# Hybrid pool/SSD decoder step: weight rings placed on 256-byte bounds, sample z values kept beside the x rows

## The reference

```
proj = einsum('bld,dk->blk', h, w_in)            # -> u | z | xBC | dt | gates
branch A = pooled(u) -> w_pool -> w_pool_br
xs, bm, cm = causal_conv(xBC);  y = ssd_chunked(xs, dt, a, bm, cm, state)
y = (y + d_skip * xs) * silu(z);  y = grouped RMSNorm(y) * ssd_norm_w
branch B = y @ w_ssd_br
merged = sigmoid(g_pool) * A + sigmoid(g_ssd) * B
x = LN(ALPHA*x + merged @ w_out);  x = LN(ALPHA*x + memory attention)
x = LN(ALPHA*x + (silu(x @ w_gate) * (x @ w_up)) @ w_down)
```

## Time and profile before

| | |
|---|---|
| median of 3 runs | 2116.43 us (2116.13 to 2117.07) |
| the profiled execution | 2115.2 us |
| its span, first to last instruction | 2113.6 us |
| PE busy | 2094.5 us, 99% |
| weight loads on PE | 2077.5 us, 98% |
| DVE, ACT, POOL busy | 1480.1, 1118.3, 162.4 us |
| granted TensorE clock | 0.997 over the span |

### The profile page before, as it was taken

How to read it: one execution, slowest core, us unless ns; L and a number is a source line. 1 busy time by engine, 2 the same in 40 slices (tenths; PEclk the granted TensorE clock), 3 DMA queues, 4 the chain that set the end, 5 groups by cost and what they waited for, 6 DMA issues and landing times.

```text
span 2113.6 us, 47660 instructions
## 1 busy us (share of the span) xinstructions
PE 2094.5 (99%) x17400; PEld 2077.5 (98%) x17400; DVE 1480.1 (70%) x2394; ACT 1118.3 (53%) x1671; POOL 162.4 (8%) x298
## 2 busy tenths in 40 slices
PE   9999999999999999999999999999999999999997
PEld 8999999999999999999999999999999999999997
DVE  8788877888788988544446876976666666545545
ACT  6566556566545545434344455666666665433333
POOL 1000000000002332000000010001111110000000
PEclk9999999999999999999999999999999999999998
DMA  7555555455557998555555575468888887555553
GB/s 284 194 172 184 189 187 184 164 184 189 186 194 245 310 290 274 178 179 180 179 180 204 178 278 209 160 220 289 281 291 285 277 286 253 172 189 180 180 181 110
DMA packets 125363, 451.78 MB, mean 214 GB/s; under 512 B 16057, under 2 KB 16313, under 8 KB 124233
## 3 DMA queue, kind: packets, MB, share of 16 engines
q1 hardware_dynamic: 101232, 366.41, 50.9%
q0 software_dynamic: 24048, 84.20, 13.0%
HBM read 427.87 MB, written 23.99 MB: 214 GB/s over the span
## 4 chain that ended last, share of the span: by engine, by line
PE 94%; DVE 3%; ACT 1%; DMA 1%; issue 1%; ACTq 0%; POOL 0%; DVEq 0%; SPq 0%
PE G L402 26%; PE G L403 26%; PE G L404 26%; PE M L402 4%; PE M L403 4%; PE M L404 4%; DVE sb_wlo L1398 1%; PE M L514 1%; PE M L526 1%; DMA sb_raw<-in_wstream 0%; ACT sb_whi L871 0%; DVE sb_resid L1682 0%; PE M L517 0%; PE M L497 0%; ACT sb_resid L1370 0%
## 5 line engine op out<-in xcount | busy, mean ns | idle before, releaser
L1398 DVE TENSOR_TENSOR sb_wlo<-sb_raw,sb_whi 128x1024 fp32r<-128x1024 f32 x688 | 834.3, 1223 | 566.0 <-ACT sb_whi L871 563.3
L871 ACT ACTIVATE sb_whi<-sb_raw 128x1024 fp32r<-128x1024 f32 x688 | 721.6, 1059 | 745.5 <-PE G L404 624.7
L402 PE MATMUL G<-sb_xH,sb_whi 128*128 128x264 f32 (+1 forms) x3072 | 871.4, 284 | 2.2 <-DVE sb_wlo L1398 1.6
L403 PE MATMUL G<-sb_xL,sb_whi 128*128 128x264 f32 (+1 forms) x3072 | 868.3, 283 | 0.0
L404 PE MATMUL G<-sb_xH,sb_wlo 128*128 128x264 f32 (+1 forms) x3072 | 867.9, 283 | 0.0
L402 PEld LDWEIGHTS G<-sb_xH,sb_whi 128*128 128x128 f32 x3072 | 577.1, 188 | 5.0 <-issue 2.5
L403 PEld LDWEIGHTS G<-sb_xL,sb_whi 128*128 128x128 f32 x3072 | 577.3, 188 | 0.0
L404 PEld LDWEIGHTS G<-sb_xH,sb_wlo 128*128 128x128 f32 x3072 | 577.2, 188 | 0.0
L403 PE MATMUL G<-sb_hL,sb_whi 128*128 128x264 f32 x704 | 200.2, 284 | 0.0
L404 PE MATMUL G<-sb_hH,sb_wlo 128*128 128x264 f32 x704 | 199.7, 284 | 0.0
L402 PE MATMUL G<-sb_hH,sb_whi 128*128 128x264 f32 x704 | 199.3, 283 | 0.0
(11 more groups left out here) (383 smaller groups left out, 2955.5 us busy)
## 6 DMA issues: line engine op xcount, KB each, us to landing
sb_raw<-in_wstream SPq DMA_DIRECT2D x688, 512.0 KB, 4.1
sb_st<-in_state_ssd POOLq DMA_DIRECT2D x32, 512.0 KB, 5.9
out_new_ssd_s<-sb_st POOLq DMA_DIRECT2D x32, 512.0 KB, 3.8
sb_tmp<-in_state_ssd POOLq DMA_DIRECT2D x34, 256.0 KB, 5.1
sb_cumbc<-scr_cum POOLq DMA_DIRECT2D x8, 1024.0 KB, 5.0
sb_resid<-in_state_ssd POOLq DMA_DIRECT2D x30, 256.0 KB, 4.4
sb_kc<-in_kc POOLq DMA_DIRECT2D x8, 512.0 KB, 8.2
sb_vc<-in_vc POOLq DMA_DIRECT2D x8, 512.0 KB, 6.1
```

The lines of the kernel that those rows point to most:

```text
L402: pe.matmul(out, w, kH, start=start, stop=False)
L403: pe.matmul(out, w, kL, start=False, stop=False)
L871: act.activation(whi[:, slot, :], raw[:, slot, :], ACT.Copy).then_inc(hi_ready, 1)
L1398: dve.tensor_tensor(wlo[:, slot, :], raw[:, slot, :], whi[:, slot, :].bitcast(F32), ALU.subtract)\
```

## The change

The three weight rings move up by 128 bytes, so that every tile in them begins at 0 modulo 256; another 128 bytes are left free behind them, so that x rows keep their place at 128 modulo 256. Everything behind moves by 256 bytes and keeps its place modulo 256. The 256 bytes are found by taking away `zsamp` as a tensor (1,024 bytes): its values go to columns `GAP + 32` to `GAP + 47` of the `xL` rows, the last 16 of the 320. The DVE copy and the DVE multiply that touch it take the layout of `dtxc` and `decc`.

```diff
+        alloc(ctx, "before_weights", [P, 32])
         raw = alloc(ctx, "raw", [P, RING, UNIT])
         whi = alloc(ctx, "whi", [P, RING, UNIT], F32R)
         wlo = alloc(ctx, "wlo", [P, RING, UNIT], F32R)
+        alloc(ctx, "before_x", [P, 32])
...
+        zsamp = planes[:, KT:2 * KT, GAP + 8 * XPG:GAP + 12 * XPG]
...
-        xsamp, zsamp, tails, bcp = overlay(
-            KEEP, xsamp=([P, SG, XPG],), zsamp=([P, SG, XPG],), tails=([P, CT, 11],), bcp=([P, SG],))
-        CS, prod = overlay(KEEP + 2 * XPG * SG * 4, CS=([P, SG, XPG],), prod=([P, XPG, P],))
-        (rc,) = overlay(KEEP + 3 * XPG * SG * 4 + 3 * P * 4, rc=([P, 4, 16],))
+        xsamp, tails, bcp = overlay(
+            KEEP, xsamp=([P, SG, XPG],), tails=([P, CT, 11],), bcp=([P, SG],))
+        CS, prod = overlay(KEEP + XPG * SG * 4, CS=([P, SG, XPG],), prod=([P, XPG, P],))
+        (rc,) = overlay(KEEP + 2 * XPG * SG * 4 + 3 * P * 4, rc=([P, 4, 16],))
...
-                        dve.tensor_copy(rows(zsamp), zs[:, :, SEQ:T])
+                        dve.tensor_copy(own_rows(zsamp), zs[:, :, SEQ:T].rearrange("p i (r b) -> p i r b", r=2))
...
-            dve.tensor_tensor(CS[:, :, :], CS[:, :, :], zsamp[:, :, :], ALU.mult).then_inc(s["sy_ready"], 1)
+            dve.tensor_tensor(cs_rows, cs_rows, zsamp[:, :, :], ALU.mult).then_inc(s["sy_ready"], 1)
```

More of the change, by code:

```diff
@@ L1588, in group @@
                 gr = t["g"].now() * 2
-                own_rows = dtxc[:, gr:gr + 2, :] if isinstance(gr, int) else dtxc[:, bass.ds(gr, 2), :]
-                dve.tensor_tensor(own_rows.rearrange("p r (b i) -> p i r b", i=XPG),
+                own_rows = (lambda x: x[:, gr:gr + 2, :].rearrange("p r (b i) -> p i r b", i=XPG)) if isinstance(gr, int) else (
+                    lambda x: x[:, bass.ds(gr, 2), :].rearrange("p r (b i) -> p i r b", i=XPG))
+                dve.tensor_tensor(own_rows(dtxc),
                                   sl[:, :, 0:NSAMP].rearrange("p i (r b) -> p i r b", r=2),
```

## The result

The changed kernel takes 2135.03 us (median of 4 runs, 2134.78 to 2135.63), the kernel before beside it 2116.28 us (4 runs, 2115.76 to 2117.07): 18.75 us more, ratio 1.0089 with a 95% interval of 1.0077 to 1.0101. It is slower, by two thirds of what I forecast.

A forecast was written before the change was run, and what follows sets the result against it. PE, busy 99% of the span, was taken as the bound. The profiled 2115.2 us plus 27.5 for x plus 0 gave 2142.7, with the median 1.2 above: 2144 us, 1.3% slower; range 2091 to 2155, the forecast's own 2125 to 2161.

The forecast's parts named there:

- The bound: Whole kernel: PE is busy 99% of the span, so time is the number of matmuls times the distance between their starts.
- What counts is the place against the weight tile: Main forecast for x matmuls: rows half of 256 bytes from the weight tiles stream slower; 2144 us, chance 0.48.
- y's slow rows moved four along: Sign in y's matmuls: rows 1 and 2 become slow, 5 and 6 fast, the average staying 122.5 ns.
- The rival of the row's own place: Rival for x: only the moving row's place modulo 256 counts, so the time stays 2116.4 us; chance 0.13.
- that of the tile's own place: Rival: weight tiles at 0 touch fewer 256-byte pieces, so y, mix and h gain too; 2100 us, sharing 0.39 for faster.
- The rule: PE's weight and row ports are independent, so the weights' place could not change x's streaming: median 2116.4 us.
- The price, 123.3 ns: Time per x matmul after the change, taken from y row 6 (row at 0, weights at 128).
- The term, 27.5 us: Added time for x: 10,560 matmuls times 123.3 less 120.7 ns.
- the base: x's time per matmul before the change, taken as 120.7 ns for all, with the input projection in the middle.
- settles in a rhythm: Condition for being wrong: x at one place for thousands of matmuls finds a rhythm that six matmuls of y never show.
- y, mix and h at nothing, mem below 1 us: Other PE matmuls: y, mix and h taken as 0, bound 6 us either way; 384 of memH and memL, 1 us.
- The helping rival, 2091 us: Rival for x: streams meet less often, x goes at 118.3 ns, -25 us; faster by either way had chance 0.39.

The follow-up runs named there:

- both_zero: The changed kernel without the second 128-byte gap, so weight tiles and x rows both begin at 0 modulo 256; 2116.07 us against 2115.72 for the kernel before.
- probe_map: The kernel before plus 65 unused stretches of 96 matmuls, at 64 pairs of high-row and low-row distances from the weight tiles; 128/128 ran at 120.0 ns per matmul.
- probe_leads: The kernel before plus unused 48-matmul stretches, varying distance, length of the small matmul ahead, and width; distance 128 showed 120.0 and 123.3 ns per matmul.
- x_at_64: The changed kernel with the second padding shortened: weight tiles at 0, x rows at 64 modulo 256; 2115.96 us in one run, where 2121 was expected.
- probe_history: The kernel before plus unused stretches at distance 128 or 0, behind stretches at other distances or small matmuls; at 128, 120.0 ns behind distance 0, 123.3 behind 32.
- x_at_192: The changed kernel with the second padding lengthened: weight tiles at 0, x rows at 192 modulo 256; 2111.72 us, ratio 0.9978 to the kernel before.

## Why the prediction was right, and where a term was off

**The bound.** Right: the pace of PE's matmuls is all. Of 19.6 us in the span, x has 22.0 and everything else less than nothing; ACT, DVE and SP cost nothing in their new place: PE waits 4.1 us, and DVE and ACT are as busy as before.

**What counts is the place against the weight tile.** Right, and shown in both directions: y's slow rows moved four along, behind its first lap; both at 0 brought the time back (2116.07 us); the loss is not in the z values (2115.62 us). The rival of the row's own place (2116.4 us) falls with the result itself, since the x rows had kept theirs; that of the tile's own place (2100 us) falls with both_zero, where the tiles lie as in the changed kernel and the loss is gone. That the traffic of other engines on the moved rings might be the cause, which the prediction did not name, falls with the probes.

**The rule.** The Trainium skill, TensorE: Matmul & The Clock Gate, Part 2, says that the weight load takes no read bandwidth from the running matmul. The prediction drew from it that the weights' place could not matter, and this case's traces show that it does: moving the weight tiles by 128 bytes made x of the gate and up stage 3.3 ns slower, at the same clock and the same operands. The measurement decides; by the rule the median was to be 2116.4 us, and 2135.03 was measured.

**The price, 123.3 ns.** Gate and up runs at 123.3, and the x of a branch round takes 11.83 us (forecast 11.84). That it came out to the digit is in part luck. The 123.3 was a difference of two starts rounded to 0.01 us; by the exact starts that row of y takes 123.8. And a row in passing is no measure of a steady pace: at 192 the rows of y take 124.8 ns and x 120.1, at 96 they take 125.4 and x mostly about 126.5. At 128 the two happened to lie close, and x was mostly at the slow one of its two paces, where one stretch of probe_map and one of probe_leads went at 120.0.

**The term, 27.5 us.** This is the one that was off; it measured 22.0. Two halves. I gave 123.3 ns to all 10,560 matmuls, but a distance of 128 has a second pace: 95 or 96 of the 408 units of x went at 120.0 and 312 at 123.0 to 123.5, a mean of 122.54 for the 264-column ones. And the base: I took 120.7 as a middle, and it was 120.47, since about 268 of the 408 units were at 120.0 before. With both means, of 266-column matmuls too (122.23 to 124.44), the term is 20.3 + 1.7 us. That x "settles in a rhythm" was named as what could make the prediction wrong; it took about a quarter of the x units.

**y, mix and h at nothing, mem below 1 us.** Right in size: -0.5 us together, and -0.5 us for mem. (They are 5,376 matmuls, not the 5,600 of the prediction.)

**The helping rival, 2091 us.** It fell: x did not go faster at this place. Its evidence, the 118.3 ns of one row of h, does not last: no steady pace at 264 columns was below 119.9 in 64 pairs. But the idea that x could meet a better partner than its like was true in small: at 192, 2111.72 us, because there x is at 120.0 nearly always, where at 0 a third of it is at 121.0 to 121.5.

**What is open.** What in the chip makes the distance matter was only argued (two streams that read the same memory and meet); no run looks into it, and the widths of probe_leads do not support it. That the past picks the pace is shown in the probes; in the real kernel it is argued from them, and which pace a stage gets could not be foretold; hence the miss of x_at_64. In both_zero half of the 266-column units go at 126.7 ns, where the probe gives only 122.1 to 122.4 at distance 0: a second pace again, and what picked it was not followed.

## What to carry to other kernels

Where PE is busy 99% of the span and reloads its weights for each matmul, count starts in a window to get the time from one matmul to the next, and compare stages that stream rows from different places: here the start of the row minus that of the weight tile, modulo 256 bytes, set x to between 120.0 and 126.7 ns and the kernel to between 2111.7 and 2158.4 us, with no instruction changed. Aligning to a round number is no aim in itself: tiles and rows both at 0, and both at 128, gave the same time; look for a distance that shows the good pace behind everything that you put ahead of it (192 here), and try it in the kernel, since a short probe can show one pace of several.

## What the runs showed of the hardware that I had not expected

- The same stream has several steady paces, and what ran before it picks one: 120.0 or 123.3 ns at distance 128 and 120.0 or 121.2 at 0 (probe_history), 121.7 or 126.7 at 96 (probe_leads), 120.0 or 121.0 at 64 (x_at_64). They can last for thousands of matmuls (3,244 starts in 400 us at 123.3, 3,158 at 126.7).
- Over columns divided by 2.4, a matmul with its weight load took 10 to 16 ns more at distance 0, from 264 columns (120.0 ns, its faster pace) to 448 (202.7). The extra does not shrink as the columns grow.
- The lowest pace seen depends on the width: 120.0 ns in the fastest steady stretches of 264 columns, but a mean of 114.5 for mem's 256 columns as moving rows in x_at_192.
